# Masking, maximum and division in the softmax of a top-k attention: one fused VectorE instruction with an additive mask, the division on ScalarE

## The reference

```
att = einsum('bqhd,bqnd->bqhn', qb, k_sel) * HEAD_DIM_2 ** -0.5
att = where(valid[:, :, None, :], att, -1e30)
p = softmax(att, axis=-1)
return einsum('bqhn,bqnd->bqhd', p, v_sel)
```

## Time and profile before

| | |
|---|---|
| time, median of 3 runs | 1579.8 us (1579.7 to 1580.3) |
| span of the profiled execution, first to last instruction | 1577.3 us |
| TensorE busy, share of the span | 1418.1 us, 90% |
| VectorE busy | 1121.3 us, 71% |
| ScalarE busy | 618.1 us, 39% |
| GpSimd busy | 403.3 us, 26% |
| DMA | 435.95 MB, 276 GB/s in the mean |

### The profile page before, as it was taken

The page is one execution under the profiler, slowest core; times in us unless marked ns, Lnnn a source line. Parts: engine busy times, 40 slices in busy tenths (PEclk is TensorE's granted clock), DMA queues, the critical chain, the costliest instruction groups (busy, mean ns, idle before and its releaser), DMA issues.

```text
span 1577.3 us, 19688 instructions
## 1 busy us (share of the span) xinstructions
PE 1418.1 (90%) x7237; PEld 1050.6 (67%) x7237; DVE 1121.3 (71%) x2287; ACT 618.1 (39%) x1353; POOL 403.3 (26%) x385
## 2 busy tenths in 40 slices
PE   8899999999999999999999998888887777777777
PEld 6688888889888999999889994333333333333322
DVE  3876775557876687777898778677777666666754
ACT  4222122213566444445565654333333333333322
POOL 0000010001200100011006236544454444444440
PEclk9999999999999999999999999999999998999999
DMA  8754585445642366555545589999999999999996
GB/s 323 272 191 143 167 287 191 159 138 171 209 147 67 121 201 187 170 176 170 160 134 163 197 330 401 420 421 422 422 421 422 420 422 421 421 422 421 422 422 282
DMA packets 86191, 435.95 MB, mean 276 GB/s; under 512 B 9488, under 2 KB 13584, under 8 KB 53072
## 3 DMA queue, kind: packets, MB, share of 16 engines
q0 software_dynamic: 45024, 298.08, 46.9%
q1 hardware_dynamic: 41072, 136.62, 26.8%
HBM read 433.61 MB, written 1.05 MB: 276 GB/s over the span
## 4 chain that ended last, share of the span: by engine, by line
PE 63%; DMA 15%; DVE 15%; ACT 4%; issue 1%; POOL 1%; SPq 0%; ACTq 0%; DVEq 0%; POOLq 0%
PE ps L585 15%; PE ps L586 15%; PE ps L587 15%; PE ps L1005 13%; DMA HF<-in_puv,AB 8%; DMA WF<-in_puv,AB 4%; DMA work<-in_puv,AB 2%; DVE WR L1411 2%; DVE work L2248 1%; PE ps L623 1%; DVE HF L2248 1%; PE ps L764 1%; ACT L1386 1%; DVE ring L2248 1%; ACT WR L1025 1%
## 5 line engine op out<-in xcount | busy, mean ns | idle before, releaser
L585 PE MATMUL ps<-HR,WR 128*128 128x256 f32 (+2 forms) x1224 | 389.1, 318 | 8.5 <-DVE WR L1411 6.9
L586 PE MATMUL ps<-HR,WR 128*128 128x256 f32 (+2 forms) x1224 | 384.4, 314 | 0.0
L587 PE MATMUL ps<-HR,WR 128*128 128x256 f32 (+2 forms) x1224 | 384.4, 314 | 0.0
L1411 DVE TENSOR_TENSOR WR<-ring,WR 128x1024 fp32r<-128x1024 f32 (+1 forms) x245 | 285.6, 1172 | 118.7 <-ACT WR L1025 117.2
L1025 ACT CAST WR<-ring 128x1024 fp32r<-128x1024 f32 (+1 forms) x245 | 241.8, 993 | 291.7 <-PE ps L587 291.6
L585 PEld LDWEIGHTS ps<-HR,WR 128*128 128x128 f32 x1224 | 233.7, 191 | 26.1 <-issue 7.3
L586 PEld LDWEIGHTS ps<-HR,WR 128*128 128x128 f32 x1224 | 233.8, 191 | 14.0 <-issue 0.2
L587 PEld LDWEIGHTS ps<-HR,WR 128*128 128x128 f32 x1224 | 233.6, 191 | 14.0
L585 PE MATMUL ps<-AR,WR 128*128 128x256 f32 (+1 forms) x535 | 165.4, 309 | 0.9 <-DVE AF L1818 0.9
L586 PE MATMUL ps<-AR,WR 128*128 128x256 f32 (+1 forms) x535 | 164.9, 308 | 0.0
L587 PE MATMUL ps<-AR,WR 128*128 128x256 f32 (+1 forms) x535 | 164.9, 308 | 0.0
(11 more groups left out here) (335 smaller groups left out, 2245.3 us busy)
## 6 DMA issues: line engine op xcount, KB each, us to landing
AB<-in_w_adaT POOLq DMA_DIRECT2D x56, 512.0 KB, 4.6
ring<-in_f1i SPq DMA_DIRECT2D x44, 512.0 KB, 4.6
ring<-in_f2i SPq DMA_DIRECT2D x44, 512.0 KB, 3.6
ring<-in_w SPq DMA_DIRECT2D x29, 512.0 KB, 3.5
ring<-in_f1o SPq DMA_DIRECT2D x21, 512.0 KB, 3.9
ring<-in_f2o SPq DMA_DIRECT2D x16, 512.0 KB, 3.6
ring<-in_wq SPq DMA_DIRECT2D x16, 512.0 KB, 4.4
ring<-in_w_ada SPq DMA_DIRECT2D x12, 512.0 KB, 9.1
```

The lines of the kernel that those rows point to most:

```text
L585: e.matmul(o, l[0], r[0], start=first, stop=False)
L586: e.matmul(o, l[0], r[1], start=False, stop=False)
L587: return e.matmul(o, l[1], r[0], start=False, stop=last)
L1411: e.tensor_tensor(WS[:, m % NSP, 1, 0:nk * cols], ring[:, ring_of(m) % NS, 0:nk * cols], WS[:, m % NSP, 0, 0:nk * cols].bitcast(F32), ALU. ...
```

## The change

The mask is now added: line 1979 gives 0 for a chosen key and -BIG otherwise. One `tensor_tensor_reduce` takes the place of line 2079 and the reduction: it writes (scores + mask) times the query's factor into `P2` and the maximum of the row into `small`. The negation stays. The division leaves VectorE: of `div`, VectorE keeps the reciprocal, and ScalarE, which had nothing in this entry, multiplies the row block by it, in place. TensorE's transpose waits for ScalarE instead of VectorE. `row_max` and `row_scale` go, as nothing else calls them.

```diff
--- before.py
+++ after.py
@@ -914,7 +914,7 @@
                              start=True, stop=True).then_inc(*mm.to("s2", s[1]))
                 elif s[0] == "pt":
                     o = bank("pt2", s[1])
-                    q.wait_ge(*dv.at("p2", s[1]))
+                    q.wait_ge(*ac.at("p2", s[1]))
                     for k in range(items2[s[1]][1] + 1):
                         x = e.transpose(o[:, 128 * k:128 * k + 128], P2[:, s[1] % 4, 128 * k:128 * k + 128], K("ident"))
                     x.then_inc(*mm.to("pt2", s[1]))
@@ -1310,6 +1310,12 @@
                     q.wait_ge(*dv.at("nm2", n))
                     e.activation(P_, P_, ACT.Exp, bias=small[:, c + 1:c + 2], scale=1.0,
                                  accum_out=small[:, c + 2:c + 3]).then_inc(*ac.to("exp2", n))
+                elif s[0] == "div":
+                    n = s[1]
+                    c = 4 * (n % 8)
+                    P_ = P2[:, n % 4, 0:KEYS[items2[n][1]]]
+                    q.wait_ge(*dv.at("rsum", n))
+                    e.activation(P_, P_, ACT.Copy, scale=small[:, c + 3:c + 4]).then_inc(*ac.to("p2", n))
                 elif s[0] == "pt":
                     hd, i = items2[s[1]]
                     n = i + 1
@@ -1680,19 +1686,6 @@
                 q.wait_ge(*ac.at("root", *key))
                 e.scalar_tensor_tensor(out=X, in0=X, scalar=gain, in1=r, op0=ALU.mult, op1=ALU.mult).then_inc(
                     *dv.to("scaled", *key))
-
-            def row_max(n, src, scale, name):
-                c = 4 * (n % 8)
-                e.reduce_max(small[:, c:c + 1], src, AX).then_inc(*dv.to("max", name, n))
-                q.wait_ge(*dv.now())
-                e.tensor_scalar(small[:, c + 1:c + 2], small[:, c:c + 1], -scale, None, ALU.mult).then_inc(
-                    *dv.to("nm" + name, n))
-
-            def row_scale(n, P_, name):
-                c = 4 * (n % 8)
-                e.reciprocal(small[:, c + 3:c + 4], small[:, c + 2:c + 3]).then_inc(*dv.to("rsum", name, n))
-                q.wait_ge(*dv.now())
-                e.tensor_scalar(P_, P_, small[:, c + 3:c + 4], None, ALU.mult).then_inc(*dv.to("p" + name, n))
 
             def raw_low(d):
                 q.wait_ge(*ac.at("raw hi", d))
@@ -1976,7 +1969,7 @@
                     q.wait_ge(*dv.now())
                     e.tensor_tensor(sl, sl, w_, ALU.add).then_inc(*dv.to("ties", i))
                     q.wait_ge(*dv.now())
-                    e.tensor_scalar(sl, sl, 2 * BIG, -BIG, ALU.mult, ALU.add).then_inc(*dv.to("ties", i))
+                    e.tensor_scalar(sl, sl, BIG, -BIG, ALU.mult, ALU.add).then_inc(*dv.to("ties", i))
                     q.wait_ge(*dv.now())
                     e.tensor_tensor(sl, sl, cap, ALU.min).then_inc(*dv.to("sel", i))
 
@@ -2076,14 +2069,15 @@
                     if n >= 4:
                         q.wait_ge(*mm.at("pt2", n - 4))
                     P_ = P2[:, n % 4, 0:w]
-                    e.scalar_tensor_tensor(out=P_, in0=bank_of("s2", n)[:, 0:w], scalar=rq[:, 4 * i + hd:4 * i + hd + 1],
-                                           in1=sel[:, i, 0:w], op0=ALU.mult, op1=ALU.min).then_inc(*dv.to("ps", "s2", n))
-                    q.wait_ge(*dv.now())
-                    row_max(n, P_, 1.0, "2")
+                    e.tensor_tensor_reduce(P_, bank_of("s2", n)[:, 0:w], sel[:, i, 0:w], rq[:, 4 * i + hd:4 * i + hd + 1], -3e38,
+                                           ALU.add, ALU.max, small[:, c:c + 1]).then_inc(*dv.to("ps", "s2", n))
+                    q.wait_ge(*dv.now())
+                    e.tensor_scalar(small[:, c + 1:c + 2], small[:, c:c + 1], -1.0, None, ALU.mult).then_inc(*dv.to("nm2", n))
                 elif s[0] == "div":
                     n = s[1]
+                    c = 4 * (n % 8)
                     q.wait_ge(*ac.at("exp2", n))
-                    row_scale(n, P2[:, n % 4, 0:KEYS[items2[n][1]]], "2")
+                    e.reciprocal(small[:, c + 3:c + 4], small[:, c + 2:c + 3]).then_inc(*dv.to("rsum", n))
                 elif s[0] == "stat":
                     for c in range(2):
                         s_, bn = st[:, 8 * c:8 * c + 8], bnb[:, 6 * c:6 * c + 6]
```

## The result

| | before | after |
|---|---|---|
| time, median of 15 runs each | 1579.75 us | 1577.38 us |
| ratio, 95% interval | | 0.9984 (0.9978 to 0.9991) |
| span of the profiled execution | 1577.3 us | 1575.0 us |
| first mask to second z product | 29.46 us | 26.87 us |
| first mask to first gather | 111.33 us | 108.75 us |

The last two lines of the table are distances inside one profile, from the first mask (step 14) to the start of the second z product and to the start of the first gather. They serve in all that follows, as they are far steadier than the time; what happens ahead of the first mask is not in them. The first mask starts between 802.39 and 806.18 us in thirteen profiles, and that spread is what comes before it.

The account below looks back on a forecast made before the run. VectorE was taken to set the time up to 829 us, TensorE behind 833. Four rounds at 0.63 us saved 2.5 us from 1577.3 span, giving 1574.8 span and 1577.3 us time; range 1575.9 to 1580.0.

Parts of the forecast that it names:

- The bound and the sum: VectorE sets the time up to 829 us; four masks and four divisions at 0.63 us a round save 2.5 us.
- The fused instruction: 128-wide half on VectorE: mask to negation falls from 0.70 to an estimated 0.38 us, saving 0.32 us each.
- The division: Steps 15 to 18: leaving VectorE, it cuts 0.39 us from reciprocal to next mask to 0.08, saving 0.31 us each.
- The pitch of 0.07 us: On VectorE the mask follows the reciprocal it does not need this closely, as read from negation at 808.63, next at 808.70.
- The sentence of the Trainium skill: Next VectorE operation waits until the pipe is empty: mask about 0.19 us behind the reciprocal, sum 2.1 us.
- Margin in step 16: Tightest place on ScalarE: weight cast done at 812.28, VectorE's line 1411 reached at 812.58, 0.25 us to spare after hand-over.
- The root's margin of 0.15 us: Step 18: ScalarE's work through the root takes 3.4 us, VectorE's 3.55, so VectorE still sets line 2102.
- the third rival: Each division brings two 1.28 us table loads on ScalarE; about +9 us, 1588.8 us; chance 0.05 with its like.
- The transposes: TensorE's transposes wait for ScalarE, 0.7 us behind the reciprocal's start instead of 0.62; the last at 818.1, 2.1 us earlier.
- What is late next: GpSimd's gain and offset pair ahead of the second z product: ends at 830.6, TensorE arrives at 829.6, waits 1 us.
- The second rival: GpSimd's line 2309 escapes VectorE's long reciprocal, 1.06 us more go: -3.6 us, 1576.2 us; chance 0.13.
- about 4 us: Most to be had, from TensorE's unfilled time from 800 to 850 us: 4.0 us, 0.26% of the kernel.

Follow-up runs that it names:

- the two single edits: Two kernels, each with one half against the kernel before: fused instruction only, ratio 0.9993; division on ScalarE only, ratio 0.9994.
- the last experiment: Changed kernel without negation, second normalization moved to step 19, long reciprocal and its root to step 6: 1575.91 us against 1579.72 before, ratio 0.9973.
- the kernel with the root early: Changed kernel without negation, VectorE's long reciprocal and its ScalarE root moved from step 20 to step 6: ratio 0.9986 to the kernel before.

## Why the prediction was right

- **The bound and the sum.** 2.5 us were predicted and 1577.3; 2.59 us at z, 2.58 at the first gather, and 1577.38 were measured. That the time agrees to 0.1 us is luck in part: its interval allows a gain of 1.4 to 3.5 us. What bears the mechanism out is the distances, and the two single edits. The raw position of the z product moved by 2.29 only (830.96 from 833.25), because the first mask of that profile started 0.30 us later; over all thirteen profiles that start varies by 3.8 us. So positions of two profiles are not to be compared; distances inside each repeat to a hundredth or two.
- **The fused instruction.** Estimated 0.38 us to the negation from a 1024-wide one, measured 0.39; saved 0.31 per item (0.32). The scale from a column and the PSUM input cost nothing that shows.
- **The division.** 0.31 us was predicted for each; alone it brought 1.36 / 4 = 0.34 on the way to z. The pitch of 0.07 us between reciprocal and mask came out as read from two other instructions.
- **The sentence of the Trainium skill** (VectorE: DVE Perf Modes, "The DRAIN you can't avoid"), by which the sum would be 2.1 us, is contradicted, taken alone, by this pitch and by the sum. The same section goes on that a next operation that is not held starts earlier, which I had left out; the pitch of 0.07 us agrees with that.
- **ScalarE.** Margin in step 16, from the end of the cast to line 1417: 0.30 predicted (812.28 to 812.58; 0.25 after the hand-over), 0.31 measured. The root's margin of 0.15 us held: the root was done 0.17 us before line 2096 started, and this line did not wait. The run with longer ScalarE work shows that these were real limits. ScalarE has no table load at line 1318 in the whole execution, so the third rival falls.
- **The transposes.** The prediction's rounds and its 0.7 us put them at 807.9, 811.4, 814.4 and 818.1; with the 0.30 us of that profile added, 808.2, 811.7, 814.7 and 818.4; measured 808.27, 811.66, 814.72 and 818.28.
- **What is late next.** GpSimd's pair, 1.0 us predicted, 1.1 measured.
- **What was missed.** From step 22 on VectorE waits for ScalarE's casts (0.34 us at 833.90 and again at 837.61), which I had not listed, and the two subtractions behind these waits take 2.12 and 2.10 us instead of 1.22. TensorE is full there, so it cost nothing. The second rival's neighbour was wrong, as shown above. And about 4 us was given as the most that can be had, while the last experiment had 4.35: the idle times understate a wait. A matmul's end is modelled 0.16 us behind the start of its successor in a full stream (0.28 us long, 0.12 apart), so a wait of 0.84 us, as in the earlier trace rows, holds TensorE up by about 1.0. With 0.16 for each, the five waits before are 4.84 us and the one that was left 0.34.

## What to carry to other kernels

Find the engine whose queue sets the stage, and price an edit from start to start of its instructions, not by busy time: two kinds of saving then simply add, until the next engine's order (here the weight cast behind the division) comes within its margin. Check that margin as a number, because it says how much more may be moved. And a wait that is visible on the critical engine may hide another right behind it: removing it paid nothing until the bank that was freed late behind it was dealt with as well.

## What the runs showed of the hardware

- Behind a fused instruction 128 wide (0.34 us, with an accumulator read of 0.08 after it), an instruction that does not need the accumulator starts 0.28 us after the fused one, and one that needs it 0.39 us after.
- VectorE and GpSimd hold each other up when both read two SBUF tensors: VectorE's 256-wide operations go from 0.48 and 0.42 to 1.52 and 1.47 us, GpSimd's 512-wide ones from about 1.3 to between 2.1 and 2.4 us. Beside VectorE's one-input reciprocal GpSimd's took 1.29.
- It is mostly one of the two that pays, and the start decides. In the kernel before, a subtraction of VectorE begun at 836.61 kept its 1.22 us, and GpSimd's line 2314, begun at 836.77, took 2.21. In the changed kernel GpSimd began at 833.65 and kept 1.29, and the subtraction begun at 833.90 took 2.12.
- One input alone does not protect: line 1979 of the kernel before, a `tensor_scalar` with one SBUF input, 256 wide, took 1.28 us beside GpSimd's offset; line 1962, of the same kind and width, took 0.34 with GpSimd idle.
- One idle spell of TensorE of 1.77 us was followed, 0.9 us after it, by about 3.4 us at a granted clock of 0.50, the 1.2 GHz level. Spells of 1.43 to 1.45 us in other kernels near that place were not, nor was one of 1.73 us at z in the kernel with the root early. What else decides is open; it was not tried.
